# A kernel of delta rule, attention and experts on one core: more gathers of experts in the second block's delta rule

## The chip, the core and the metric

The kernel runs on one core of a Trainium2 chip. The core has a matrix engine (TensorE, in the profile PE), a vector engine (VectorE, DVE), a scalar engine (ScalarE, ACT), GpSimd (POOL), a queue engine (SyncE, SP), and 16 DMA engines that move data between main memory and the on-chip memory. The metric is the time of one execution on the device in microseconds, the median of several.

## What is computed

One layer over 1024 tokens of width 1024, float32. Its core, cut from the reference:

```python
proj = h @ w_in
y_a = _gdn_branch(gq, gk, gv, gz, ga, gb, ...)      # conv, delta rule in chunks, gated norm
y_b = _fox_branch(fq, fk, fv, ff, f_bias, w_out_fox)  # attention with forget gates, causal
mix = sigmoid(gate_a) * y_a + sigmoid(gate_b) * y_b
h = _layernorm(DEEPNORM_ALPHA * h + mix @ w_o, ln1_g, ln1_b)
h = _layernorm(DEEPNORM_ALPHA * h + _peer(h, peer_wq, peer_keys, peer_u, peer_v), ln2_g, ln2_b)

# _peer: each token chooses 8 heads x 16 = 128 of 16384 experts by top-k of product keys
u = jnp.take(u_tab, e_blk, axis=0)
act = jax.nn.gelu(jnp.einsum('td,tkd->tk', h_blk, u)) * g_blk
vv = jnp.take(v_tab, e_blk, axis=0)
return jnp.einsum('tk,tkd->td', act, vv)
```

Each of the 1024 tokens reads 128 rows of `u_tab` and 128 rows of `v_tab`, 4 KB each: 1.07 GB in all.

## The kernel before

**Blocks and units.** The sequence is worked on in four blocks of 256 tokens (`T`, `NB`), each two tiles of 128. What a block needs is cut into units, and `order()` (line 48) writes them out in one list, `UNITS`, of 548 pairs of a name and a number. For a block `b` they are: the projections (`sm`, `sv`, 13 `conv`, `z`, `rT`, `fqk`, `fv`); the delta rule (`nrm`, then for each of two chunks of 128 tokens `prod`, six levels `lev`, `wu`, `ws`, `o`, and `og`); attention (17 times `att` and `ato`, then `ot`); the merge (8 `mix`, 4 `wo`, 2 `ln`); and the choosing of the experts (8 heads, each two `top`, a `cand` and a `sel`, then `idx`). From block 1 on the delta rule, attention and merge of a block follow each other, and the projections of block `b + 1` stand between the units of the choosing of block `b`. Every engine walks through `UNITS` in the same order and does its part of each unit; semaphores tie them together.

**The experts beside it.** The experts of a block are worked on while later blocks are computed. A *dot* is one gather of 128 rows of `u_tab` (one expert choice of each token of a tile, 0.5 MB) by POOL, line 640, and one operation of VectorE that multiplies the rows with `h_cur` and sums them, line 999 (shown as a custom operation and a short read of the accumulator). A tile has 128 dots, the kernel 1024. A *token* is one gather of the 128 rows of `v_tab` of one token, line 652; TensorE sums four tokens at once with 8 matrix multiplications of 512 columns, line 1312. There are 1024 tokens too. Tokens of a tile may begin only when all its dots are done, its activations are made and turned over (line 1302).

**The ring.** Both kinds of gather write into a ring of 15 places (`NR`). POOL issues them in one fixed order and waits at each for the place to be free, that is, for the dot or the four tokens that used it 15 places before. So POOL runs at most 15 gathers ahead of VectorE and TensorE. Before a dot of a new head POOL also waits for that head's choice (`s_sel`, raised by line 1281 in `sel`). Between a unit's own instructions and the next unit's, VectorE does the unit's dots and TensorE its tokens, in order, waiting for each row to arrive.

**The table.** `pace()` (line 93) decides before the program is built how many dots (`DOTS`) and tokens (`TOKS`) stand behind each unit. Up to `idx` of block 0 dots are given out evenly. From there up to the last block's choosing, each unit has a share, `SHARE[kind]`, a guess of how long it takes, made larger for attention of later blocks by `share()`; the dots of that part of the program are handed out in proportion to the shares' running sum, so all shares together always receive the same number of dots. The result is cut off at what has been chosen: no dot of a block is placed before the unit `sel` of its second head, and 16 more with each further `sel`; no more than 8 dots follow a unit:

```python
            run += share(kind, b) if n < alone else 0.0
            want = base + round((T * (NB - 1) - base) * run / total)
        dots.append(max(dots[-1], min(want, ready, dots[-1] + 8)))
```

Tokens follow the dots at a distance of `P + LAG` = 136, in fours. The remaining units' table, and the part behind the last block's choosing, come from the same function.

Of the kernel before, what the change touches and what calls it, by code (L numbers as in the profile page):

```python
# [48 lines left out]
def order():  # L49
# [19 lines left out]
    for b in range(NB):  # L69
# [4 lines left out]
        for n, (kind, i) in enumerate(CHOOSE):  # L74
# [9 lines left out]
SHARE = {"sm": 1.0, "sv": 7.0, "nrm": 6.0, "conv": 3.5, "z": 5.0, "rT": 1.5, "fqk": 3.5, "fv": 5.0, "prod": 12.0, "lev": 5.0, "wu": 4.0,  # L84
         "ws": 3.0, "o": 4.0, "og": 8.0, "att": 2.5, "ato": 1.5, "ot": 4.0, "mix": 9.0, "wo": 6.0, "ln": 9.0,
         "top": 3.5, "cand": 6.5, "sel": 6.5, "idx": 3.0}


def share(kind, b):
    return SHARE[kind] * (1.0 + 0.7 * b if kind in ("att", "ato") else 1.0)  # L90


def pace():

    first = UNITS.index(("idx", 0, 0))
    last = UNITS.index(("idx", NB - 1, 0))
    alone = UNITS.index(("top", NB - 1, 0))
    total = sum(share(kind, b) for kind, b, i in UNITS[first + 1:alone])
    dots, toks = [0], [0]
    ready, run, lately = 0, 0.0, 0  # L100
    for n, (kind, b, i) in enumerate(UNITS):

        if kind == "sel":
            ready, lately = T * b + TOPK * i, 0
        if kind == "idx" and b:
            ready = T * (b + 1)
        if n == first + 1:
            ready, base = T, dots[-1]
        lately += 1
        if n <= first:  # L110
            want = max(0, ready - TOPK) + round(TOPK * lately / 7) if ready else 0
            want = min(want, P - 8)
        else:
# [4 lines that stand above are left out]
# [1579 lines left out]
```

How the kernel before makes its waits and increments, by code:

```python
            def sm_(b, i):  # L434
                sp.wait_ge(s_proj, projected(b, "sm", 0))
                next_items(b, 0, 1)
# [1 line left out]
            def conv(b, c):  # L438
                if c < 12:
                    sp.wait_ge(s_proj, projected(b, "conv", c))
                    next_items(b, 1 + c, 1)
                if b == 0 and c in (9, 11):
                    fetch("gt", (c - 9) // 2)
                if c == (3 if b else 9):
                    sp.wait_ge(s_rows, b + 1)
                    sp.dma_start(d_rows[:, b * T:(b + 1) * T], rows).then_inc(s_rowst, 16)
# [1 line left out]
            def z(b, i):  # L449
                sp.wait_ge(s_proj, projected(b, "z", i))
                next_items(b, 13 + 2 * i, 2)
# [1 line left out]
            def fqk(b, c):  # L453
                sp.wait_ge(s_proj, projected(b, "fqk", c))
                next_items(b, 17 + c, 1)
# [7 lines left out]
            def rT(b, i):  # L463
                sp.wait_ge(s_rowst, 16 * (b + 1))
                for j in range(2):
                    sp.wait_ge(s_mix[j], 4 * b)
                gates(TT * b)
# [1 line left out]
            def gt(b, m):  # L469
                i, k = divmod(m, 2)
                if k:
                    sp.wait_ge(s_gb2[i % 2], i // 2 + 1)
                    if i + 2 < 8:
                        fetch("gt", i + 2)
                    elif i == 7:
                        fetch("wo", 0)
# [1 line left out]
            def prod(b, c):  # L478
# [5 lines left out]
                    fetch("mix", 0)  # L484
                if c == 0 and b:
                    sp.wait_ge(s_proj, PB * (b + 1))
                    fetch("mix", 1)
```

## Time and profile before

| | us |
|---|---|
| median of 3 runs | 3906.41 |
| lowest, highest | 3903.19, 3912.52 |
| the profiled execution | 3916.44 |
| its span | 3914.4 |

The profile is of one execution, 10 us above the median. The span goes from the first to the last instruction, and windows are cut in it by times from its start. Busy times are sums over an engine's instructions; the DMA share is the mean busy share of the 16 DMA engines; a gather is one DMA on queue q0. Some shares stand at 1.01 to 1.03, since they are made from the packets' own times.

### The profile page before, as it was taken

To read this page: it belongs to the slowest core of one execution; us is meant where nothing else is said; L and a number is where in the kernel's file an instruction comes from. 1 tells how busy PE (TensorE), PEld (TensorE's weight loads), DVE (VectorE), ACT (ScalarE), POOL (GpSimd) and SP (SyncE) were. 2 spreads that over 40 slices of the span, in tenths; PEclk is the share of its full clock that TensorE was granted. 3 is DMA by queue.
4 is the path that set the end of the run, shared out by engine and by line. 5 is a ranking of instruction groups with operands and counts; after the bars stand their busy time and mean duration, and the time that the engine had idled before them with its cause. 6 is when DMAs were issued, how large, how long until landed. Compare 5 with 4: busy or idle time off the path is not lost.

```text
span 3914.4 us, 36529 instructions
## 1 busy us (share of the span) xinstructions
PE 2497.4 (64%) x11992; PEld 1538.0 (39%) x11992; DVE 2256.2 (58%) x5313; ACT 533.9 (14%) x1224; POOL 2304.5 (59%) x2086
## 2 busy tenths in 40 slices
PE   8788864567967876557967866556787710132354
PEld 6675752434735533334635533323554300000010
DVE  5243899754468776654368776555446668544300
ACT  3220310211003202111003202111101000000000
POOL 1000455367656666677556766577666677777765
PEclk9898987776988988777988988767898855555577
DMA  5213788599998999899998999899999999999998
GB/s 174 77 68 146 278 327 284 167 329 379 412 365 341 374 408 369 295 367 365 415 365 346 406 408 342 296 359 343 376 412 381 381 327 369 362 358 363 362 368 319
DMA packets 367619, 1290.18 MB, mean 330 GB/s; under 512 B 39468, under 2 KB 68148, under 8 KB 362308
## 3 DMA queue, kind: packets, MB, share of 16 engines
q0 software_dynamic: 294912, 1073.87, 72.6%
q1 hardware_dynamic: 66760, 201.39, 14.0%
q10 hardware_dynamic: 5760, 12.59, 0.8%
q8 instruction: 97, 1.59, 0.2%
q14 instruction: 90, 0.74, 0.0%
HBM read 1274.72 MB, written 12.98 MB: 329 GB/s over the span
## 4 chain that ended last, share of the span: by engine, by line
PE 26%; POOL 22%; DVE 15%; issue 14%; DMA 10%; another core or an unknown queue 7%; DVEq 3%; ACT 3%; SPq 0%; ACTq 0%; POOLq 0%
POOL ring L640 12%; POOL ring L652 11%; PE banks L1323 10%; DMA ring<-in_ev,idxT 8%; DVE ring L999 7%; PE banks L1312 5%; PE banks L1333 4%; PE banks L1588 2%; PE banks L1534 1%; PE banks L1373 1%; PE banks L1328 1%; PE banks L1514 1%; DVE arena L951 1%; DVE arena L953 1%
## 5 line engine op out<-in xcount | busy, mean ns | idle before, releaser
L640 POOL DMA_INDIRECT ring<-in_eu,eidx x1024 | 1188.2, 1160 | 1121.7 <-DVE eidx L1281 397.8
L999 DVE CUSTOM_DVE_ANT_0 ring<-ring,h_cur 128x1024 f32<-128x1024 f32 x1024 | 1216.7, 1221 | 293.1 <-DMA ring<-in_eu,eidx 266.3
L652 POOL DMA_INDIRECT ring<-in_ev,idxT x1024 | 1104.5, 1079 | 465.8 <-issue 298.2
L1312 PE MATMUL banks<-ring,wide 128*32 128x512 f32 x4096 | 718.2, 832 | 630.8 <-DMA ring<-in_ev,idxT 539.9
L1323 PE MATMUL banks<-arena,wslot 128*128 128x256 f32 (+1 forms) x3248 | 758.7, 391 | 64.5 <-ACT arena L752 30.2
L1323 PEld LDWEIGHTS banks<-arena,wslot 128*128 128x128 f32 (+1 forms) x3248 | 626.7, 195 | 229.4 <-issue 121.8
L1312 PEld LDWEIGHTS banks<-ring,wide 128*32 128x32 f32 x4096 | 146.5, 135 | 1045.3 <-issue 1003.5
L1333 PE MATMUL banks<-arena 128*128 128x128 f32 x1408 | 225.4, 321 | 55.0 <-ACT arena L801 30.5
L1333 PEld LDWEIGHTS banks<-arena 128*128 128x128 f32 x1408 | 205.9, 229 | 86.5 <-ACT arena L801 39.4
L1328 PE MATMUL banks<-ident,arena 128*128 128x128 f32 x216 | 50.9, 393 | 177.2 <-DVE arena L970 52.1
L1323 PE MATMUL banks<-ring,wslot 128*128 128x256 f32 (+1 forms) x656 | 152.3, 389 | 11.4 <-DMA wslot<-in_w_sm 7.0
L1534 PE MATMUL banks<-arena 128*128 128x64 f32 x528 | 93.5, 343 | 78.8 <-ACT arena L852 43.2
L982 DVE SCALAR_TENSOR_TENSOR h_cur<-h_cur,banks 128x512 f32<-128x512 f32 x16 | 10.3, 682 | 224.4 <-PE banks L1312 200.5
L1323 PEld LDWEIGHTS banks<-ring,wslot 128*128 128x128 f32 (+1 forms) x656 | 126.4, 196 | 30.1 <-issue 11.9
L1534 PEld LDWEIGHTS banks<-arena 128*128 128x128 f32 x528 | 85.7, 251 | 124.0 <-issue 72.4
L1200 DVE TENSOR_TENSOR arena<-arena,banks 128x256 f32<-128x256 f32 x48 | 18.1, 419 | 197.7 <-issue 91.9
L1173 DVE RECIPROCAL rinv<-rsum 128x1 f32<-128x1 f32 x64 | 10.5, 164 | 208.7 <-PE banks L1534 132.8
L1302 PE MATMUL banks<-ident,wgt 128*128 128x128 f32 x8 | 2.7, 342 | 196.8 <-issue 193.1
L1328 PEld LDWEIGHTS banks<-ident,arena 128*128 128x128 f32 x216 | 36.4, 201 | 201.0 <-DVE arena L970 60.2
L1588 PE MATMUL banks<-wslot,arena 128*128 128x512 f32 x256 | 113.5, 601 | 1.5 <-issue 1.5
L1514 PE MATMUL banks<-arena 65*128 65x512 f32 (+3 forms) x160 | 87.5, 670 | 29.3 <-DMA arena<-d_fv 25.6
L945 DVE MAX8 arena<-arena 128x8 f32<-128x128 f32 (+1 forms) x192 | 55.4, 289 | 73.0 <-ACT arena L897 64.4
(231 smaller groups left out, 2387.6 us busy)
## 6 DMA issues: line engine op xcount, KB each, us to landing
wslot<-in_w_pq SPq DMA_DIRECT2D x64, 576.0 KB
wslot<-in_w_mix SPq DMA_DIRECT2D x24, 1536.0 KB
wslot<-in_w_qkv SPq DMA_DIRECT2D x48, 512.0 KB
wslot<-in_w_fqk SPq DMA_DIRECT2D x32, 512.0 KB
wslot<-in_w_out SPq DMA_DIRECT2D x8, 2048.0 KB
ring<-in_eu,eidx POOLq DMA_INDIRECT x1024
ring<-in_ev,idxT POOLq DMA_INDIRECT x1024
wslot<-in_w_z SPq DMA_DIRECT2D x16, 512.0 KB
```

Source lines behind the costliest of these rows:

```text
L640: pool.indirect_dma_start(out=ring[:, UPOS[k] % NR, :], out_offset=None, in_=eu, in_offset=bass.IndirectOffsetOnAxis(ap=eidx[:, n % (2 * T ...
L652: pool.indirect_dma_start(out=ring[:, VPOS[k] % NR, :], out_offset=None, in_=ev, in_offset=bass.IndirectOffsetOnAxis(ap=idxT[:, n % (2 * T ...
L945: dve.max(v16[:, 0:8], vals)
L951: dve.max(v16[:, 8:16], vals)
L999: dve.tensor_tensor_reduce(out=row, in0=row, in1=h_cur[:, n % 3, :], scale=1.0, scalar=0.0, op0=ALU.mult, op1=ALU.add, accum_out=dots[:, n ...
L1312: last = pe.matmul(BY[k][32 * j:32 * j + 32, :], wide32[:, at:at + 32], ring[:, VPOS[4 * q + j] % NR, k * 512:(k + 1) * 512], start=(m == ...
L1323: last = pe.matmul(bank, w[:, k0 + k, :], rhs[:, k, :], start=(k == 0), stop=(k == nk - 1))
L1328: last = pe.transpose(bank[:, h * P:(h + 1) * P], src[:, h, :], ident[:, :])
L1333: last = pe.matmul(bank[:, h * P:(h + 1) * P], lhs[:, h, :], rhs[:, h, :], start=True, stop=True)
L1514: last = pe.matmul(SB[b][r][:, k0:k1], qa[b][0:FD + 1, j, qt * P:(qt + 1) * P], kh[b][0:FD + 1, i % 2, j, k0:k1], start=True, stop=True)
L1534: last = pe.matmul(TB[b][0][:, 0:FD], pT[b][:, k, :], vh[b][:, i % 2, k, FD * j:FD * (j + 1)], start=(k == 0), stop=(k == nk - 1))
L1588: last = pe.matmul(B[4 + tt][:, :], mixT[:, k, tt * P:(tt + 1) * P], w[:, k, :], start=(k == 0), stop=(k == KB - 1))
```

## The change

`share()` multiplies the shares of six kinds of units by 1.8 where the block is block 1: `prod`, `lev`, `wu`, `ws`, `o` and `og`, which is all of the delta rule but `nrm`.

```diff
 def share(kind, b):
+    if b == 1 and kind in ("prod", "lev", "wu", "ws", "o", "og"):
+        return SHARE[kind] * 1.8
     return SHARE[kind] * (1.0 + 0.7 * b if kind in ("att", "ato") else 1.0)
```

Since this raises the total, the rest gets a little less. All computed work is the same; the units' order is the same; what changes is behind which unit dots and tokens stand, and with it the order of POOL's gathers and the places in the ring. The tables, by stage:

| stage | units | dots, tokens before | dots, tokens after |
|---|---|---|---|
| up to `idx` of block 0 | 177 | 101, 0 | 101, 0 |
| block 1: delta rule with `nrm` | 23 | 49, 12 | 81, 44 |
| block 1: attention | 35 | 45, 44 | 43, 44 |
| block 1: merge | 14 | 43, 44 | 31, 32 |
| block 1: choosing, with block 2's projections | 61 | 101, 100 | 105, 104 |
| block 2: delta rule | 23 | 48, 48 | 46, 44 |
| block 2: attention | 35 | 64, 64 | 60, 60 |
| block 2: merge | 14 | 43, 44 | 41, 44 |
| block 2: choosing, with block 3's projections | 61 | 101, 100 | 96, 96 |
| block 3: delta rule | 23 | 48, 48 | 46, 44 |
| block 3: attention | 35 | 82, 84 | 77, 76 |
| block 3: merge | 14 | 43, 44 | 41, 44 |
| behind it | | 256, 392 | 256, 392 |

The cut at what has been chosen now takes hold in two places. Behind the third `wo` of block 1 the table has 256 dots, all of block 0; it has no dot and no token behind the next 14 units, up to block 1's second `sel` (before: 27 dots and 28 tokens). Until block 1's choosing ends the table then has 16 dots with each `sel`, 8 behind it and 8 behind the unit after it for most heads, and tokens in fours behind these two units and the two after them, then nothing to the next `sel`. In block 2 the 512th dot stands behind the first `cand`, the next 8 units have none, and for three heads the dots stand bunched in the same way.

TensorE, block 1's delta rule from the second chunk's `prod` on. L1333 (L1335 in the changed program, whose lines lie two further on) is a level's multiplication, L1302 turns the activations of tile 0 over, L1312 (L1314) is four tokens. Before:

```order
L1333 MATMUL banks<-arena 128x128 x36
L1302 MATMUL banks<-ident,wgt 128x128
L1312 MATMUL banks<-ring,wide 32x512 x8
L1333 MATMUL banks<-arena 128x128 x16
L1312 MATMUL banks<-ring,wide 32x512 x8
L1333 MATMUL banks<-state,arena 128x128 x4
```

and now:

```order
L1335 MATMUL banks<-arena 128x128 x8
L1304 MATMUL banks<-ident,wgt 128x128
L1314 MATMUL banks<-ring,wide 32x512 x8
L1330 MATMUL banks<-ident,arena 128x128 x4
L1335 MATMUL banks<-arena 128x128 x12
L1314 MATMUL banks<-ring,wide 32x512 x8
L1335 MATMUL banks<-arena 128x128 x12
L1314 MATMUL banks<-ring,wide 32x512 x8
L1330 MATMUL banks<-ident,arena 128x128 x4
```

The first tokens stand six units earlier, behind the second `prod`, and a group of four stands behind all but one of the units from there to the end of the delta rule, eleven in all where there were three.

VectorE, from the last `wo` of block 1 into its first `ln`. L1210 (L1212) adds the output projection, L957 to L970 (L959 to L972) are the layer norm, L999 (L1001) a dot, L989 (L991) the gates on tile 1's activations. Before:

```order
L1210 SCALAR_TENSOR_TENSOR arena<-arena,banks 128x512
L999 ISA ring,dots<-ring,h_cur 128x1024
L999 ISA dots 128x1
L999 ISA ring,dots<-ring,h_cur 128x1024
L999 ISA dots 128x1
L957 BN_STATS arena<-arena 128x6 x2
L959 BN_AGGR arena<-arena 128x2
L961 TENSOR_SCALAR arena<-arena 128x1
L964 RECIPROCAL arena<-arena 128x1
L966 TENSOR_SCALAR arena<-arena 128x1024
L968 TENSOR_TENSOR arena<-arena 128x1024
L970 TENSOR_TENSOR arena<-arena 128x1024
```

and now:

```order
L1212 SCALAR_TENSOR_TENSOR arena<-arena,banks 128x512
L991 TENSOR_TENSOR wgt<-wgt,gate 128x128
L959 BN_STATS arena<-arena 128x6 x2
L961 BN_AGGR arena<-arena 128x2
L963 TENSOR_SCALAR arena<-arena 128x1
L966 RECIPROCAL arena<-arena 128x1
L968 TENSOR_SCALAR arena<-arena 128x1024
L970 TENSOR_TENSOR arena<-arena 128x1024
L972 TENSOR_TENSOR arena<-arena 128x1024
L959 BN_STATS arena<-arena 128x6 x2
L961 BN_AGGR arena<-arena 128x2
```

The dots behind `wo` are gone, and the norm of the first tile is followed by that of the second with no dots between.

## Rows read from the trace of the kernel before

**Rows 1.** The page: span, DMA slices, the gathers' queue, issues of L640
```profile
span 3914.4 us, 36529 instructions
...
DMA  5213788599998999899998999899999999999998
...
q0 software_dynamic: 294912, 1073.87, 72.6%
...
L640 POOL DMA_INDIRECT ring<-in_eu,eidx x1024 | 1188.2, 1160 | 1121.7 <-DVE eidx L1281 397.8
```

**Rows 2.** Windows at the stages: engines' busy us, clock, DMA share, GB/s
```profile
core 0: us, PE busy (x) PEld busy (x) DVE busy (x) ACT busy (x) POOL busy (x), PEclk, DMA share, GB/s
679.00:830.00 151.00, 86.22 (x489) 69.83 (x489) 107.00 (x198) 36.48 (x80) 71.08 (x57) 0.76 0.61 203
830.00:960.00 130.00, 94.84 (x384) 44.83 (x384) 72.88 (x155) 21.02 (x54) 99.18 (x89) 0.63 1.00 374
...
1201.00:1477.00 276.00, 213.97 (x973) 132.07 (x965) 206.45 (x598) 52.08 (x130) 183.88 (x164) 0.89 0.98 385
1477.00:1647.00 170.00, 102.44 (x632) 69.49 (x632) 106.52 (x196) 37.26 (x81) 113.29 (x100) 0.80 0.90 328
...
2523.00:2783.00 260.00, 153.00 (x757) 79.12 (x761) 130.52 (x240) 40.36 (x76) 181.62 (x159) 0.72 0.94 339
```

**Rows 3.** Windows: the two halves of block 1's delta rule
```profile
679.00:747.00 68.00, 40.73 (x224) 33.81 (x224) 51.17 (x90) 16.18 (x36) 32.09 (x24) 0.80 0.58 185
747.00:830.00 83.00, 45.49 (x268) 36.01 (x265) 55.83 (x109) 20.30 (x45) 38.99 (x33) 0.73 0.64 218
```

**Rows 4.** Timeline, a level step: VectorE, then gather issues on POOL
```profile
717.05 0.69 DVE L1126 TENSOR_TENSOR arena<-arena,banks 128x512 f32<-128x512 f32 x1
...
718.85 1.22 DVE L999 CUSTOM_DVE_ANT_0 ring<-ring,h_cur 128x1024 f32<-128x1024 f32 x1
...
720.00 1.22 DVE L999 CUSTOM_DVE_ANT_0 ring<-ring,h_cur 128x1024 f32<-128x1024 f32 x1
...
721.32 0.69 DVE L1126 TENSOR_TENSOR arena<-arena,banks 128x512 f32<-128x512 f32 x1
...
718.06 0.94 POOL L640 DMA_INDIRECT ring<-in_eu,eidx  x1 [0.30 <-issue]
720.35 1.68 POOL L640 DMA_INDIRECT ring<-in_eu,eidx  x1 [1.35 <-DVE dots L999]
```

**Rows 5.** POOL in block 1's second prod; window with VectorE at rest
```profile
758.82 1.68 POOL L640 DMA_INDIRECT ring<-in_eu,eidx  x1 [10.46 <-DVE dots L999]
...
3800.00:3900.00 100.00, 52.40 (x280) 10.89 (x272) 0.00 (x0) 0.00 (x0) 62.37 (x67) 0.72 0.97 366
```

**Rows 6.** Timeline of VectorE: wo and sel of blocks 0 and 1
```profile
358.63 0.69 DVE L1210 SCALAR_TENSOR_TENSOR arena<-arena,banks 128x512 f32<-128x512 f32 x1 [6.18 <-PE banks L1588]
...
445.60 0.18 DVE L1281 SCALAR_TENSOR_TENSOR eidx<-arena 128x32 uint32<-128x32 f32 x1
...
672.79 0.18 DVE L1281 SCALAR_TENSOR_TENSOR eidx<-arena 128x32 uint32<-128x32 f32 x1
...
1091.67 0.69 DVE L1210 SCALAR_TENSOR_TENSOR arena<-arena,banks 128x512 f32<-128x512 f32 x1 [2.74 <-PE banks L1588]
...
1206.44 0.19 DVE L1281 SCALAR_TENSOR_TENSOR eidx<-arena 128x32 uint32<-128x32 f32 x1
...
1470.57 0.18 DVE L1281 SCALAR_TENSOR_TENSOR eidx<-arena 128x32 uint32<-128x32 f32 x1
```

**Rows 7.** Windows before the second sel, blocks 0, 0, 1 and 2
```profile
337.00:412.00 75.00, 59.75 (x206) 38.41 (x207) 29.19 (x87) 6.37 (x12) 0.00 (x0) 0.89 0.37 138
412.00:446.00 34.00, 24.27 (x102) 20.36 (x101) 27.32 (x93) 14.07 (x36) 14.36 (x15) 0.90 0.84 317
1092.00:1206.00 114.00, 74.72 (x356) 47.03 (x349) 86.48 (x230) 17.07 (x36) 63.54 (x56) 0.82 0.88 342
2007.00:2089.00 82.00, 55.95 (x273) 38.18 (x272) 63.89 (x194) 14.48 (x30) 44.70 (x41) 0.83 0.85 331
```

## The prediction

> **What bounds the kernel now.** I read the page first: the DMA slices and the queues [rows 1]. The gathers of expert rows (queue q0, 2048 of 0.5 MB each) take 72.6% of 16 engines' span, the DMA slices stand at 9 or more for most of the run, and no compute engine does. 72.6% of 3914.4 us over 2048 gathers is 1.39 us of all 16 DMA engines for one gather; that price carries the sum. The chain of waits mixes the vector engine, the gathers and the matrix engine, so I did not sum by it.
>
> Then the windows, cut at the program's stages [rows 2]. Where the share is about 1.0 the transfers set the time: block 1's attention (89 gathers in 130 us, 1.46 us each with the key and value loads) and the choosing of block 1 (0.98). The delta rule of block 1 is the exception: 61 gathers (49 dots, 12 tokens by the table; POOL, running ahead, has 57 in the window) in 151 us, share 0.61. Cut in two [rows 3], its halves have 0.58 and 0.64, so the engines idle 68 x 0.42 = 28.6 us and 83 x 0.36 = 29.9 us. As the bytes of the program don't change, the change in time is the change in the DMA engines' idle time, as long as some stretch stays transfer-bound. That is the account I keep; a sum stage by stage stands beside it.
>
> **The change, part by part.** The table puts 32 more dots and 32 more tokens into the delta rule of block 1; every one is taken from a later stage. Nothing else is added.
>
> *First half of the delta rule* (units nrm to o of chunk 0): 36 dots instead of 22, no tokens. In a level step the vector engine is nearly full: three operations of 0.6 to 0.7 us and two dots, 4.27 us from one L1126 to the next [rows 4], so a third dot of 1.15 us (start to start of consecutive dots, [rows 4]) comes on top. In prod it waits for the norm and some are hidden. 14 x 1.15 = 16 us is the ceiling, I take 11. DMA work there is 68 x 0.58 = 39.4 plus 14 x 1.39 = 19.5, in 79 us: idle 20, a gain of 9.
>
> *Second half*: 89 gathers (45 dots, 44 tokens) instead of 39. POOL enters with the ring of 15 places full and leaves some 8 places short, so about 81 x 1.39 = 113 us of transfers fall here, more than the 83 us there are. The second prod's wait for its gate rows stays, with the ring full and POOL waiting 10.46 us for a dot [rows 5]: some 10 us idle, and 4 for gaps. POOL itself costs more here. A gather's issue takes 0.94 us where VectorE does its small operations and 1.68 under dots [rows 4], with 0.30 between issues, and 62.37 / 67 = 0.93 where VectorE does nothing [rows 5]. With 45 dots of 1.15 us in some 130 us, 40% of the time is under dots: 0.94 + 0.4 x 0.74 + 0.30 = 1.54 us an issue, 81 of them 125 us, 12 more than their transfers. Part of that runs during the wait; I take 8. So 135 us, idle 22, a gain of 8. The lower bound of idle is 0, the upper is that of block 2's delta rule, 170 x 0.10 = 17, plus 10 and 12. Matrix work is no limit: eight more groups of tokens. Together the delta rule grows by 11 + 52 = 63 us and saves 17 us of idle time.
>
> *What is late next.* The dots can't run ahead of the experts chosen. All 256 dots of block 0 are now done with unit wo 2 of block 1, and dots of block 1 come no sooner than its second sel: 14 units without a gather, where 27 dots and 28 tokens stood. POOL's next gather waits for the first sel (L1281). What such a stretch looks like is in the trace, since block 0 has the same units with no gathers at all: from its third wo to its second sel 358.6 to 445.6, 87 us; in block 1 1091.7 to 1206.4, 114.8 us [rows 6]. DMA idles from where POOL has run out, 15 places or 21 us ahead of the dots. For block 0 that window, 337 to 412, has share 0.37 of weights and stores alone: idle 75 x 0.63 = 47. After the first sel POOL fills the ring, 15 gathers, and stops: 412 to 446 has exactly that, share 0.84, idle 5. Block 1 now idles 114 x 0.12 = 14 there [rows 7]. The loss is 52 - 14 = 38 us (bounds 25, if block 1's weights fill more than block 0's, and 48).
>
> *Bursts.* From there to the end of block 1's choosing the table has 16 dots and 16 tokens for each sel, in two units with 8 dots and 4 tokens each and two with 4 tokens, then four units with none. Between the second and the eighth sel are six such periods in 264 us now [rows 6], with 155 gathers. Share 0.98 x 264 = 259 less 155 x 1.39 = 215 leaves 44 us for weights. With 192 gathers: 267 + 44 = 311, less 15 fetched ahead, plus some 8 at the end: 301 us, 50 a period. The vector engine needs about 38 (six of block 0's periods, 16 dots each, take 227.2 us, from its second sel at 445.6 to its eighth at 672.8 [rows 6]), so it isn't the bound, and DMA finds a free place nearly always: between bursts it has 8 tokens and 15 dots' places to fill, 32 us of work in some 20. POOL has 32 issues of 1.24 and 16 dots over them at up to 0.74 more, 51 us a period, as long as the transfers: that and the transfers' bursts won't fit without gaps. Idle 0 to 20 more, I take 8.
>
> *Block 2's choosing* meets the ceiling too: 512 dots are done with its first cand, 508 before ln ends. Eight units have no gathers. By the same reckoning 20 us idle before its first sel and 5 after, against 82 x 0.15 = 12 now [rows 7]: a loss of 13 (5 to 20).
>
> *The stretches behind it* lose 46 gathers in all up to the last block's choosing (dots and tokens: block 2's delta rule 2 and 4, attention 4 and 4, merge 2 and 0, its choosing 5 and 4; block 3's delta rule 2 and 4, attention 5 and 8, merge 2 and 0). Where the share is 1.0 each gives back 1.39. In the delta rules it gives less: from 61 gathers in block 1 to 96 in block 2 the delta rule grows from 151 to 170 us [rows 2], some 0.53 a gather. I take 6 us as lost that way (0 to 12). From the last block's choosing on, the table is the same.
>
> *Sum*: -17 (delta rule) +38 +8 +13 +6 = **+48 us** of idle time. Stage by stage: +63 delta rule, +6 attention (89 to 87 gathers, which no longer starts with a full ring), -5 merge, -27 the stretch without gathers, +37 six periods, +10 the last units, -64 for 46 gathers later, +6 +13 as above: +39. The second counts no gaps in the bursts; I take **+41**. The profiled execution took 3916.4 us with a span of 3914.4; the median of three is 3906.4. On the median the forecast is 3947.
>
> One price could be read otherwise. The rows show 1.39 us of DMA time for a gather, and 374 GB/s at a share of 1.00 [rows 2]. The Trainium skill, DMA: Bandwidth & Descriptors, "Anatomy of one DMA", fits a transfer's time as 2.0 us plus bytes over 436 GB/s, so 1.20 us a gather beyond the fixed part; by that estimate the burst periods and the second half of the delta rule would be some 50 us cheaper and the later gathers worth 9 less, and the time would come to about 3905. No stretch of gathers alone reached that rate.
>
> **Rivals.**
> *A, faster: cheap where added, dear where removed.* If the delta rule stays bound by its chain, an added gather costs 0.53 there as between block 1 and block 2 [rows 2]: 64 x 0.53 = 34 instead of 63. The periods of choosing are 37.9 us with 16 gathers and 44 with 25.8, 0.65 a gather, so 37 more cost 24 and not 37. And block 3's attention takes 260 us for 166 gathers, 1.57 each, so 46 fewer give back 72 and not 58. That is -29 -13 -14 = -56: 3891. Against it: 89 gathers in the second half want 113 us of transfers in 83. It decides if the delta rule stays under 185 us and the periods under 48.
> *B, no change: cheap both ways.* As A, but the gathers removed give back no more than 58: 3905.
> *C, POOL becomes the bound.* If nearly every issue of the second half fell under a dot, 1.98 us each, 89 would last 176 us, 41 more than I count: 3988. Against it: dots take 40% of that time, not all. The Trainium skill, SBUF — State Buffer, "SBUF: two separate sides", says that VectorE and GpSimd share a pair of ports under an exclusive lock, held for the whole instruction when an operation reads two operands in SBUF, so that gather descriptors can't be written meanwhile. The rows agree (1.68 beside 0.94). By that rule it is the bunched dots after each sel that hold POOL up most; the sum has it with 8 us in the delta rule and within the 8 of the bursts, and without it would be some 12 us less.
> That the change doesn't move what it says is excluded by the order of instructions.
>
> **How the numbers follow.** The forecast has 0.71, A 0.12, B 0.12, C 0.05. Within the forecast the bounds of the terms (delta rule 17 us each way, first hole -13 to +10, bursts -8 to +12, second hole 8, relief 6), which won't all fall one way, give 3916 to 3980. The range must take in most of B: 3900 to 3982 leaves out about 2 in 10. A measurement of this kernel tells 0.2%, 8 us: faster 0.12, same 0.12, slower 0.76.
>
> **What would show it.** In the profile after, the delta rule of block 1 should last some 214 us with a DMA share near 0.8; a hole of 50 to 60 us should stand between the merge and the first sel of block 1 with a share below 0.5 and no POOL work; POOL should wait for L1281's successor there, 50 us or more (now it waits so only once, at the start, 397.8 us with everything before it [rows 1]); the six periods should be 50 us with a share near 1.0; the last block's choosing and the tail should be as before, only later. The forecast is wrong if the delta rule stays near 170 us, if the hole is filled by weights, or if the periods stay at 44 us.

## The result, and the profile after

| | before | after |
|---|---|---|
| median, us | 3909.47 (4 runs) | 4033.54 (4 runs) |
| lowest, highest | 3903.19, 3914.89 | 4016.74, 4041.02 |
| span of the profiled execution | 3914.4 | 4014.3 |

The change makes the kernel slower by 2.9%: ratio 1.0292, interval 1.0257 to 1.0328. The forecast was 3947 with a range that ended at 3982: the direction was right and the size was not (124 us by the medians, 41 forecast). The profile of after is of its fastest run, so the spans differ by 100 us where the medians differ by 124; what follows explains the 100.

The page of after (lines stand two further on), to be read beside [rows 1]:

```profile
span 4014.3 us, 36522 instructions
...
DMA  5214887899968999989996999899999999999998
...
q0 software_dynamic: 294912, 1073.87, 71.5%
q1 hardware_dynamic: 66760, 201.39, 14.0%
...
L642 POOL DMA_INDIRECT ring<-in_eu,eidx x1024 | 1173.2, 1146 | 1170.3 <-DVE eidx L1283 506.9
```

The bytes are the same, but 71.5% of 4014.3 us is 2870 us of gathers where it was 2842 (72.6% of 3914.4): their transfers took longer. POOL waits 507 us for choices, where it was 398. The windows of after at the stages (columns as in [rows 2]), in this order: block 1's delta rule; its two halves; attention; the stretch without gathers; from first to second sel; the six periods between block 1's second and eighth sel; block 2's choosing with the units before it:

```profile
679.00:893.50 214.50, 115.15 (x617) 79.68 (x617) 143.87 (x262) 36.41 (x80) 150.42 (x118) 0.73 0.82 286
679.00:762.00 83.00, 45.11 (x224) 37.80 (x224) 67.50 (x122) 19.40 (x40) 52.31 (x37) 0.73 0.68 224
762.00:893.00 131.00, 70.04 (x393) 41.88 (x393) 75.86 (x140) 17.01 (x41) 97.65 (x81) 0.73 0.91 325
893.50:1031.00 137.50, 89.96 (x384) 41.87 (x384) 70.73 (x152) 20.91 (x54) 103.46 (x93) 0.65 1.01 376
...
1137.00:1213.00 76.00, 61.05 (x231) 37.47 (x230) 35.15 (x98) 7.96 (x14) 0.86 (x1) 0.89 0.45 172
1213.00:1248.00 35.00, 21.52 (x95) 16.43 (x93) 27.79 (x95) 13.77 (x33) 14.31 (x15) 0.87 0.80 305
1247.00:1578.00 331.00, 209.96 (x963) 125.63 (x964) 216.81 (x611) 40.07 (x108) 209.57 (x192) 0.79 0.95 354
2113.00:2483.00 370.00, 268.15 (x1201) 169.21 (x1193) 259.02 (x769) 60.61 (x152) 204.16 (x190) 0.85 0.89 337
```

Below, stages are cut at marks that hold no dot (the vector engine's norm, output gate, merge and sel operations), so that they compare between kernels; such a cut may lie some us from the windows above. "Idle" is a stretch less the mean time that the 16 DMA engines' packets took in it.

| stage | before, us (idle) | after, us (idle) | change | forecast |
|---|---|---|---|---|
| block 1: delta rule | 143.6 (57) | 203.2 (37) | +60 | +63 |
| attention | 152.8 (0) | 164.7 (0) | +12 | +6 |
| merge to second sel | 228.3 (11) | 198.3 (50) | -30 | -32 |
| six periods of choosing | 264.1 (5) | 330.9 (17) | +67 | +37 |
| rest of it | 9.1 | 16.1 | +7 | +10 |
| block 2 and 3, to the last block's first sel | 1496 | 1482 | -13 | -45 |
| behind it | 939 | 937 | -2 | 0 |

The first three rows came within 6 us of the forecast. POOL on the timeline of after, at the stretch without gathers, shows the wait that was forecast at "50 us or more", then 15 issues without a pause, of which the second stands here, then the wait for a dot of the second sel:

```profile
1213.89 0.94 POOL L642 DMA_INDIRECT ring<-in_eu,eidx  x1 [76.02 <-DVE eidx L1283]
1215.13 0.94 POOL L654 DMA_INDIRECT ring<-in_ev,idxT  x1 [0.30 <-issue]
...
1249.15 1.68 POOL L654 DMA_INDIRECT ring<-in_ev,idxT  x1 [16.69 <-DVE dots L1001]
```

The two misses are the six periods and the return from later stages. In the periods, the waits of before (1206 to 1470) and of after (1247 to 1578), columns: what waited for what, us in total, times, longest:

```profile
PE banks L1312 <- DMA ring<-in_ev,idxT: 27.2, 5, 8.8
...
DVE ring L999 <- DMA ring<-in_eu,eidx: 23.5, 9, 6.7
```

```profile
PE banks L1314 <- DMA ring<-in_ev,idxT: 99.5, 13, 21.4
...
DVE ring L1001 <- DMA ring<-in_eu,eidx: 52.1, 18, 7.6
POOL ring L642 <- PE banks L1314: 33.9, 5, 10.1
...
POOL ring L654 <- DVE dots L1001: 24.8, 4, 16.7
```

The matrix and vector engines wait 101 us more for rows. POOL's waits for free places grow less: before, three such rows come to 41 us (20.3, 11.3 and 9.2); after, the two shown and one of 1.7 come to 60, and 16.7 of these lie ahead of the window, being the wait that ends at 1249.15. In the first period, right behind the hole, TensorE's tokens wait for rows longest:

```profile
1264.21 3.64 PE L1314 MATMUL banks<-ring,wide 128*32 128x512 f32 x16 [21.37 <-DMA ring<-in_ev,idxT]
```

### The profile page after: what moved, and what is told of

Same layout as the page of the kernel before. It is cut to its first block, busy times and chain, and to the rows that moved or that the text cites. A ratio compares the mean times of both kernels' runs of the same rounds, so it can differ in the third digit from the quotient of the medians.

```text
span 4014.3 us, 36522 instructions
## 1 busy us (share of the span) xinstructions
PE 2532.4 (63%) x11992; PEld 1554.8 (39%) x11992; DVE 2257.2 (56%) x5313; ACT 523.2 (13%) x1217; POOL 2297.8 (57%) x2086
## 3 DMA queue, kind: packets, MB, share of 16 engines
q0 software_dynamic: 294912, 1073.87, 71.5%
## 4 chain that ended last, share of the span: by engine, by line
PE 32%; POOL 20%; DVE 15%; issue 13%; another core or an unknown queue 8%; DMA 7%; DVEq 3%; ACT 2%; ACTq 0%; SPq 0%; POOLq 0%
PE banks L1325 14%; POOL ring L654 10%; POOL ring L642 10%; DVE ring L1001 7%; PE banks L1314 6%; DMA ring<-in_ev,idxT 5%; PE banks L1335 4%; PE banks L1590 2%; PE banks L1375 2%; PE banks L1536 1%; DMA ring<-in_eu,eidx 1%; PE banks L1364 1%; PE banks L1330 1%; PE banks L1516 1%
## 5 line engine op out<-in xcount | busy, mean ns | idle before, releaser
L642 POOL DMA_INDIRECT ring<-in_eu,eidx x1024 | 1173.2, 1146 | 1170.3 <-DVE eidx L1283 506.9
L1001 DVE CUSTOM_DVE_ANT_0 ring<-ring,h_cur 128x1024 f32<-128x1024 f32 x1024 | 1215.6, 1222 | 363.2 <-DMA ring<-in_eu,eidx 315.1
L1314 PE MATMUL banks<-ring,wide 128*32 128x512 f32 x4096 | 732.0, 836 | 659.2 <-DMA ring<-in_ev,idxT 596.0
L1314 PEld LDWEIGHTS banks<-ring,wide 128*32 128x32 f32 x4096 | 147.3, 136 | 1086.8 <-issue 1070.0
L1335 PE MATMUL banks<-arena 128*128 128x128 f32 x1408 | 234.9, 330 | 71.2 <-ACT arena L803 27.7
L1335 PEld LDWEIGHTS banks<-arena 128*128 128x128 f32 x1408 | 214.9, 238 | 108.0 <-issue 54.0
L984 DVE SCALAR_TENSOR_TENSOR h_cur<-h_cur,banks 128x512 f32<-128x512 f32 x16 | 10.2, 681 | 206.8 <-PE banks L1314 172.9
L1590 PE MATMUL banks<-wslot,arena 128*128 128x512 f32 x256 | 112.2, 595 | 2.9 <-issue 2.9
L1375 PE MATMUL banks<-wslot,arena 128*128 128x512 f32 x192 | 90.7, 631 | 20.1 <-ACT arena L754 20.1
```

The costliest lines, as they stand in the source:

```text
L642: pool.indirect_dma_start(out=ring[:, UPOS[k] % NR, :], out_offset=None, in_=eu, in_offset=bass.IndirectOffsetOnAxis(ap=eidx[:, n % (2 * T ...
L1001: dve.tensor_tensor_reduce(out=row, in0=row, in1=h_cur[:, n % 3, :], scale=1.0, scalar=0.0, op0=ALU.mult, op1=ALU.add, accum_out=dots[:, n ...
L1314: last = pe.matmul(BY[k][32 * j:32 * j + 32, :], wide32[:, at:at + 32], ring[:, VPOS[4 * q + j] % NR, k * 512:(k + 1) * 512], start=(m == ...
L1335: last = pe.matmul(bank[:, h * P:(h + 1) * P], lhs[:, h, :], rhs[:, h, :], start=True, stop=True)
L1375: last = pe.matmul(PN[b][tt][:, :], xTs[b][:, k, tt * P:(tt + 1) * P], w[:, kk, :], start=(k == 0), stop=(k == KB - 1))
L1590: last = pe.matmul(B[4 + tt][:, :], mixT[:, k, tt * P:(tt + 1) * P], w[:, k, :], start=(k == 0), stop=(k == KB - 1))
```

## The experiments

They ran in three groups, on chips numbered 1, 11 and 4; the number of the first result's chip isn't known. The kernel before was run in each group: medians 3769, 3775 and 3773 us, single runs 3751 to 3791, which is 3.5% less than above. Ratios are to before in the same group. e1 to e4 ran on chip 1, the copies of both kernels and the short dots on 11, e5 and the other factors on 4. There is one profile a kernel, and before's is of chip 11, so stage lengths are mostly compared across chips. How far such a comparison carries: e3_bunched has before's table up to the second sel, and its first three stages differ from before's by 2 to 5 us.

> The kernel before, once more, for its stages on the chip of these runs: each stage in the same proportion as in its first profile, the delta rule of block 1 near 0.7 of the change's.

> The change, once more, beside its variants: 1.029 times the kernel before, as first measured, within 0.005.

Before's span was 3780.1. The change's ratio was 1.021 (1.0166 to 1.0255): the loss is smaller here, 79 us by the medians, and the expectation (1.024 to 1.034) missed. All stages of the table keep their signs. In these profiles the change has (before, after): delta rule 140.7, 194.8; attention 144.0, 155.1; six periods 250.2, 308.4; blocks 2 and 3 1439, 1419.

Counted by the bytes that arrived in each stage, this is where the gathers went and what they cost there. The delta rule got 55 more and took 54 us more, 1.0 each. The stretch from merge to the second sel got 54 fewer and gave back 35 us, 0.65 each. The six periods got 28 more and took 58 us more, 2.1 each. Blocks 2 and 3 got 42 fewer and gave back 20 us, 0.5 each. The other 14 (in attention and behind the periods) took 22 us. So no place that lost gathers gave back as much for one as any place that got them took.

**Is it the hole, or the gathers beside the delta rule?** e1_local gives the delta rule as many gathers, taken from block 1's own attention and merge, so that there is no long stretch without (its table meets the ceiling for the two units before the second sel) and the periods stay nearly as even as before:

```diff
+    if b == 1 and kind in ("prod", "lev", "wu", "ws", "o", "og"):
+        return SHARE[kind] * 1.8
+    less = 0.64 if b == 1 and kind in ("att", "ato", "ot", "mix", "wo", "ln") else 1.0
+    return less * SHARE[kind] * (1.0 + 0.7 * b if kind in ("att", "ato") else 1.0)
```

> The delta rule of block 1 has 85 dots and 48 tokens beside it as in the change, but they are taken from the attention and the merge of the same block, so that 242 dots are done at its end (before 238, the change 256) and the ceiling of chosen experts is never met. Theory 1, the loss lies in the hole and the bursts that the ceiling makes: without them the filled idle time of the delta rule is a gain of some 20 us, 3885 to 3895. Theory 2, gathers in the delta rule are dear themselves (its chain is longer, VectorE's dots hold POOL up): 3935 or more, since the delta rule grows by 64 us and attention and merge give back only what their own chains allow.

Ratio 1.0127 (1.0103 to 1.0152): slower with hardly a hole, as the second theory had it. The delta rule went from 140.7 to 210.8 us, attention from 144.0 to 146.2, and from there to the second sel 235.6 us became 210.8. Attention, of before and of e1_local:

```profile
821.00:965.00 144.00, 108.32 (x452) 54.01 (x452) 78.56 (x166) 25.96 (x63) 113.47 (x99) 0.67 1.01 381
```

```profile
892.00:1039.00 147.00, 105.89 (x404) 58.52 (x404) 63.88 (x139) 26.07 (x63) 77.36 (x75) 0.59 0.91 322
```

It issues 24 gathers fewer and is not shorter; its share has fallen to 0.91. So its share of 1.0 [rows 2] didn't mean that fewer gathers would make it shorter: something else took as long. That this was attention's own chain is likely, but no run shows it by itself. The granted clock is lower in e1_local (0.59 against 0.67), and attention's own 260 matmuls kept TensorE busy for 76 us instead of 67; how much the stage would give back at the same clock is open.

**The other side of that point.** e4_hole leaves the delta rule nearly as it was (46 dots, 8 tokens) and loads attention and merge, so that the hole and the bursts are as in the change:

```diff
+    more = 1.42 if b == 1 and kind in ("att", "ato", "ot", "mix", "wo", "ln") else 1.0
+    return more * SHARE[kind] * (1.0 + 0.7 * b if kind in ("att", "ato") else 1.0)
```

> The kernel before, with 46 dots and 8 tokens in block 1's delta rule, and the attention and merge of block 1 made to take 34 dots and tokens more than now, so that the ceiling is met behind the same unit as in the change, with the same hole, the same bursts and nearly the same table behind them. Theory 1, hole and bursts are the loss and the delta rule's filling a gain of 20: 4035 to 4060, slower than the change. Theory 2, the delta rule is the loss: 3920 to 3960.

Ratio 1.0283 (1.025 to 1.0315), more than the change's 1.021; neither theory's range was met, the first was the nearer. Its attention:

```profile
822.00:1020.00 198.00, 117.73 (x516) 54.35 (x516) 95.72 (x195) 25.96 (x63) 150.71 (x132) 0.66 1.00 372
```

33 gathers more cost 54 us, 1.64 each. The delta rule is the cheaper place for them, by 0.7% of the kernel (the two intervals just touch, and the runs are of two chips). What the two kernels share is the hole and the bursts: in both the six periods and what is behind them to block 2 take more than before, 69 us in the change and 77 here. In e1_local, which shares neither, this is 7 us, and it loses less than either.

**The bursts.** e2_even is the change with the dots at the ceiling handed out two behind each unit. e3_bunched is the kernel before with block 1's dots bunched behind each sel from the third on. Its table has 137 gathers in the six periods where before has 155; most of the rest stand behind the last sel.

```diff
             want = base + round((T * (NB - 1) - base) * run / total)
+            if kind in CHOOSING and dots[-1] < want:
+                want = max(dots[-1], min(want, ready - TOPK + 2 * lately))
```

```diff
             want = base + round((T * (NB - 1) - base) * run / total)
+            if CHOSEN < n < alone and 310 > n and kind in CHOOSING:
+                behind = UNITS[n - 1][0] == "sel"
+                want = want if kind == "sel" or behind else dots[-1]
```

> The change with the same hole of 14 units, but the dots behind it are handed out two to a unit at the ceiling, not eight and eight behind each sel; tokens follow evenly. Theory 1a, the bunching makes the six periods 55 us instead of 50: they come to 50 or less and the whole is 30 to 45 us faster than the change, 3985 to 4000. Theory 1b, the load alone (32 gathers a period) makes them 55: no change against it, 4025 to 4035.

> The kernel before, with its own table up to block 1's second sel; from there to the end of block 1's choosing the same 13 dots a period are bunched behind each sel and the unit after it. Theory 1a, bunching itself costs about 5 us a period, engines taking turns: 3930 to 3945. Theory 1b, it costs nothing while there are only 26 gathers a period: 3905 to 3915.

e2_even: 1.0176 (1.0129 to 1.0223). e3_bunched: 1.0085 (1.0052 to 1.0117). The six periods in before, the change, e2_even and e3_bunched:

```profile
1201.00:1451.00 250.00, 193.28 (x917) 123.98 (x918) 197.12 (x577) 45.85 (x117) 172.90 (x157) 0.89 1.02 404
```

```profile
1230.00:1538.00 308.00, 207.49 (x977) 125.72 (x978) 217.23 (x610) 41.50 (x110) 207.72 (x191) 0.81 0.97 373
```

```profile
1232.00:1519.00 287.00, 214.80 (x971) 127.59 (x973) 217.88 (x608) 43.58 (x111) 208.52 (x185) 0.87 1.01 399
```

```profile
1200.00:1451.00 251.00, 188.95 (x886) 122.58 (x885) 185.28 (x556) 46.10 (x119) 149.00 (x142) 0.87 0.97 370
```

Of the 58 us that the periods grow, 37 remain when the same gathers are even (share 1.01: it is the transfers), and 21 are due to the bunching. The 21 show in two ways: 12 us are idle DMA time, and 9 are more time in transfers, most of it dearer gathers: 1.364 us each against 1.329 even and 1.320 before. In e3_bunched the six periods take 251.4 us, as before, but with 13 gathers fewer by the bytes: 12 us of idle DMA time came in, and a gather took 1.364 us instead of 1.320, 6 us together. So bunching cost some 18 us there too, at 23 gathers a period, 3 us a period where the first theory had 5. The price shows behind the eighth sel, 18.5 us more for the 10 gathers left over and other transfers. By the medians e3_bunched loses 30 us, within the range of the first theory; the second (no cost at 26 gathers a period) fell. The gain of e2_even over the change in the medians (1.0176 against 1.021, 13 us where 30 to 45 were expected) is within the intervals; its 21 us are read from the stage of one profile each.

TensorE's clock can be left out as the cause of the longer periods. The granted clock of the stage is lower in the change than in before (0.81 and 0.89, means over the levels of 1.2 and 2.4 GHz), but the rows have 0.212 us of busy time for a matmul in the one (207.49 for 977) and 0.211 in the other (193.28 for 917), and the stage's matmuls other than the tokens' kept TensorE busy for 146 and 148 us.

**Is it the vector engine's dots?** In b_short_dots (before) and a_short_dots (the change) a dot covers 256 of the 1024 columns; the rest of the product is left out.

```diff
-                        out=row, in0=row, in1=h_cur[:, n % 3, :], scale=1.0, scalar=0.0,
+                        out=row[:, 0:256], in0=row[:, 0:256], in1=h_cur[:, n % 3, 0:256], scale=1.0, scalar=0.0,
```

> The kernel before with each dot's operation on VectorE over 256 of the 1024 columns (the rest of the product is left out; gathers and everything else stay). VectorE's part of a dot falls from 1.22 to some 0.4 us. Theory of transfers: most stages are bound by them, the time falls by 1 to 3%. Theory of VectorE: choosing and delta rule are bound by its dots, and POOL's issues by them: over 5%.

> The change with the same short dots. If the change loses because its bunched and added dots fill VectorE and hold up POOL's issues, it is less than 1.5% slower than the kernel before with short dots. If it loses by the hole and by gathers that arrive too late for engines that work in order, it stays 2.5 to 3.5% slower than that.

Ratios to before: 0.952 (0.949 to 0.955) and 0.9714 (0.9685 to 0.9743). One over the other is 1.020, the same loss as with full dots, so it doesn't come from their length. It lies between the two ranges expected for it (under 1.5%, 2.5 to 3.5%), and the gain of before, 4.8%, between its two as well (1 to 3%, over 5%). The page of b_short_dots, POOL's issues and the dots:

```profile
L640 POOL DMA_INDIRECT ring<-in_eu,eidx x1024 | 989.4, 966 | 1164.5 <-DVE eidx L1281 397.1
...
L999 DVE CUSTOM_DVE_ANT_0 ring<-ring,h_cur 128x256 f32<-128x256 f32 x1024 | 406.6, 424 | 590.0 <-DMA ring<-in_eu,eidx 589.0
```

The mean issue is 0.966 us instead of 1.160 [rows 1]. In the delta rule of the change the issues take 1.25 us in the mean with full dots and 0.97 with short ones, and the stage grows by 54 us with the former and by 41 with the latter: POOL's hold-up and the dots' own time are at most 13 of the 54. The rest is transfers that found no idle time: they grow by 74 us with full dots and by 65 with short ones, while idle DMA time falls by only 20 and 24.

**Dots or tokens?** e5_dots_only is e1_local with the tokens of the delta rule held at 12:

```diff
+        if WAITED[0] < s <= WAITED[1] and toks[-1] >= 12:
+            ready = toks[-1]
         if toks[-1] % P == 0 and dots[s - 1] < edge:
             ready = toks[-1]
```

> Block 1's delta rule gets 85 dots as in e1_local, but its tokens stay at 12 as in the kernel before; attention has 29 dots and 64 tokens, merge 27 and 28, nothing behind changes by more than 2, and there is no unit without gathers but where the kernel before has them. e1_local (85 dots, 48 tokens) lost 53 us: its delta rule grew by 70 us, attention by 2, merge and what is before the first sel shrank by 18. Theory 1 (what is added to the delta rule costs about 1 us each whatever it is, and what is removed from attention gives nothing back): 36 dots add 25 to 35 us to the delta rule, attention has 93 gathers instead of 89 and grows by 6, merge gives back 20: 15 to 20 us slower, ratio 1.004 to 1.005. Theory 2 (the tokens are what makes the second half slow, since the matrix engine waits for rows between the level steps): the delta rule grows by 15 us or less, ratio 0.998 to 1.001. Rival (dots cost most, tokens ride along): the delta rule grows by 50 us or more and the ratio is 1.010 or above.

Ratio 1.0087 (1.006 to 1.0115), above what the first theory gave and below the rival's. Its delta rule is 172.9 us: 36 dots add 32 us, and the 36 tokens of e1_local 38 more. A dot costs 0.9 there and a token 1.05, so the first theory holds for this stage. Part of the 32 us may be TensorE: the delta rule's own matmuls kept it busy for 93 us at a granted clock of 0.67, and in before for 80 at 0.74 (in the change for 82 at 0.73). But its attention takes 177.4 us, 33 more than before where 6 were expected:

```profile
681.00:854.00 173.00, 99.45 (x486) 82.46 (x487) 139.30 (x256) 34.30 (x76) 117.23 (x86) 0.67 0.77 259
854.00:1031.00 177.00, 125.86 (x528) 61.98 (x532) 62.45 (x137) 26.10 (x63) 110.77 (x106) 0.63 0.96 358
```

The table has 93 gathers behind its units, but POOL issues 106: in the delta rule it issued 86 where the table has 97, so it left that stage with its lead spent, as in the change (109 of 125), and made it up in attention. The change issues 106 in attention too and takes 155 us. The traces settle part of the 22 us between them: by the bytes 109 gathers arrive there and 101 in the change, which with their price is 12 us, and 8 us are idle DMA time. The table has 64 tokens there instead of 44, and attention's own matmuls took 74 us instead of 63, at a granted clock of 0.63 instead of 0.69; whether either of these makes the stage longer stays open.

**How it grows.** The change's factor of 1.8 was set to 1.2, 1.4 and 0.8.

```diff
-        return SHARE[kind] * 1.8
+        return SHARE[kind] * 1.2
```

> The change with factor 1.2 in the place of 1.8: delta rule of block 1 with 57 dots and 20 tokens (8 and 8 more than before), four units without a gather ahead of the second sel, no bunching beyond the first two periods. Theory 1 (each gather beside the delta rule costs about 1 us and gives back 0.3): 16 x 0.7 = 11 us, ratio 1.003 (1.001 to 1.005), delta rule 155 us. Theory 2 (the loss begins only where the hole and the bursts are, the delta rule has free transfer time): ratio 0.996 to 1.000, delta rule below 149 us.

> Factor 1.4: delta rule with 65 dots and 28 tokens (16 and 16 more), eight units without a gather ahead of the second sel, three periods of block 1's choosing bunched, four units without in block 2. Theory 1: 32 x 0.7 = 22 us for the delta rule, some 6 for the smaller hole: ratio 1.007 (1.004 to 1.010). Theory 2 (loss from hole and bursts only): delta rule below 158 us, ratio 1.000 to 1.003. Rival (loss is a threshold of a full ring and comes with 1.8 alone): ratio below 1.000.

> The other direction, factor 0.8: delta rule of block 1 with 40 dots and 4 tokens (9 and 8 fewer), attention 46 and 44, merge 44 and 44, block 1's choosing 102 and 104, a few more in each stage behind it. Theory 1 (beside block 1's delta rule a gather costs about 1 us even at the table of before, and elsewhere it costs nothing while attention is at its own chain): faster, ratio 0.995 to 0.999. Theory 2 (the first gathers beside the delta rule are nearly free, its 0.61 share being real free time, and those that move behind it cost 1.39 each): slower, 17 x (1.39 - 0.5) = 15 us, ratio 1.002 to 1.006.

| factor | gathers beside the delta rule | delta rule, us | six periods, us | blocks 2 and 3, us | ratio |
|---|---|---|---|---|---|
| 0.8 | 44 | 130.0 | 256.3 | 1448 | 1.0042 (1.002 to 1.0064) |
| before | 61 | 140.7 | 250.2 | 1439 | 1 |
| 1.2 | 77 | 154.9 | 264.7 | 1425 | 1.0038 (1.0021 to 1.0056) |
| 1.4 | 93 | 171.2 | 287.7 | 1423 | 1.0068 (1.0047 to 1.0089) |
| 1.8 | 125 | 194.8 | 308.4 | 1419 | 1.021 (1.0166 to 1.0255) |

With 1.2 and 1.4 the first theory held in size, and with 1.2 in the delta rule's length. With 0.8 it fell and the second held (1.002 to 1.006 expected): the 17 gathers taken out give back 11 us in the delta rule, 0.6 each, and the periods, what is behind them and the later blocks take 24 more. So of the five values tried the kernel before has the lowest time, and the loss grows slowly at first: 0.4% with a hole of four units and 2.1% with one of 14. Blocks 2 and 3 return less and less of what is moved ahead of them: 14 us for the first 14 gathers (1.2), 16 for 23 (1.4), 20 for 46 (1.8).

## Why the prediction missed

**What held.** The delta rule was to grow by 63 us with a share near 0.8, and grew by 60 with 0.82. Its two halves were put at 79 and 135 us, and windows of 83 and 131 show them. The stretch from merge to the second sel was to shrink by 32 and shrank by 30; its hole has share 0.45, where below 0.5 was forecast, and POOL's wait of 76 us is there. The idle DMA time was to grow by 48; summed over all packets it grew from 486 to 541 us, by 55. The rivals are ruled out: A and B needed the delta rule under 185 us, C needed 176 in its second half, which took 131.

**The premise that failed: "the change in time is the change in the DMA engines' idle time".** The same bytes took 45 us more of DMA time (3429 to 3474 us over all packets); on the page q0 accounts for 28 of them and q1 for 14. The prediction put this term at nothing. It is the largest part of the miss: the profiled executions differ by 100 us where 41 were forecast, and of the 59 between, 45 are dearer transfers, 7 are idle time beyond the 48, and 7 are the step from the sum of 48 down to 41. The prediction priced every gather at one mean, 1.39 us. By stage, before, it is 1.34 in the periods, 1.37 in attention, 1.43 in block 2's delta rule and 1.57 beside block 1's, where the queue is least full. The rows showed it: 57 gathers at 0.61 of 151 us [rows 2] are 1.6 each. The change moves gathers from the first kind of place to the last, and makes the good places dearer: the periods' gathers went to 1.40 and block 2's from 1.32 to 1.38, some 20 us together. In the experiments the bunched periods were dearer than the even ones by 0.035 a gather. What in the transfers takes the longer time isn't settled. In these runs gathers are dearer in stages where the queue runs empty and is then filled at once; that the one causes the other wasn't tested.

**The six periods, 331 us instead of 301.** Two terms. I took 15 gathers off as "fetched ahead" and put some 8 on at the end; but each period ends with the ring filled for the next, as it began, and the window has 192 issues, all that the table gives. Their transfers with the weights' took 314 us where I had about 301. And in the sum stage by stage I counted no gaps: idle time there is 17 us, 12 more than before, within the bounds of the first sum (0 to 20), and left out of the second, which the forecast followed. Here the step that failed is "DMA finds a free place nearly always". A place comes free only when its dot is done or its four tokens are summed, and both wait in order: POOL waited 16.7 us for a dot at the second sel, and the tokens behind it 21 us for their rows [the rows of 1249.15 and 1264.21 above].

**The return, 13 us instead of 45.** Attention of blocks 2 and 3 did give back for 21 gathers: 23 us here, 27 in the experiments' copies, where the price of 1.39 gives 29. The delta rules did not: 6 gathers fewer in each of two gave back nothing in sum here (+4 and -3); they had some 18 us of idle time each. I had 6 us for that. Block 2 from its last wo to block 3's nrm grew by 22 us (14 in the copies) where the forecast, 13 less 12.5 for its 9 gathers, had none. The 106 us from wo to the second sel, with the hole in them and fewer gathers, became 90, but its six periods grew by 40, 18 of them idle DMA time: for three heads the dots stand bunched as in block 1, and I had priced the hole alone.

**And the median.** The medians differ by 24 us more than the profiled executions. Runs of the changed kernel lie up to 24 us apart, of before in the experiments up to 37 on one chip, and the part behind the last sel, with the same table in every kernel, took 708 to 733 us there with full dots. What makes the runs differ, and whether the 24 us are more than that, stays open.

**What the share said.** I read 0.61 as free room that could take gathers at the cost of the other engines' waits. e1_local shows the account with hardly a hole: 70 us more in the delta rule, 18 less from attention to the first sel, and 9 less in blocks 2 and 3. In the copies 55 more gathers brought 74 us of DMA time into the delta rule, and only 20 of these came out of its 55 us of idle time. Idle DMA engines are no free room where the rows' own operations stand in order among those of the stage: the tokens alone made TensorE wait 26 us for rows in the delta rule of the change, and none in before. And a stretch at 1.0 need not get shorter with fewer gathers.

**The other price of a gather.** The prediction gave an estimate of 1.20 us a gather, worked out from the fit (2.0 us plus bytes over 436 GB/s) of the Trainium skill, DMA: Bandwidth & Descriptors, "Anatomy of one DMA", and with it 3905. No stage of over 30 us came under 1.30 in any run, so the measurement decides against it. The Trainium skill, SBUF — State Buffer, "SBUF: two separate sides", says that a VectorE operation with two inputs in SBUF and a GpSimd operation that reads SBUF lock one pair of ports against each other for the whole instruction. The short dots agree with it: issues of gathers, which read their indices from `eidx`, fell from 1.16 to 0.97 us in the mean when the operation beside them was a third as long. But the loss of the change didn't depend on it.

## What to carry to other kernels

Before gathers are moved into a stretch whose DMA engines idle, price both places by their own rows (share times length over the gathers in it), and ask of the place they leave whether its own chain is nearly as long: if it is, a share of 1.0 promises no return. Where work is bounded by what has been chosen, running ahead of the choice turns into a stretch with none and a crowded one behind it: here the first gave back 0.65 us for each gather that it lost, and the second took 2.1 for each that it got, 1.4 when they were spread evenly. Count a ring's lead at both ends of a window, and never take the sum that leaves out the gaps when another one has them.

## What the runs showed of the hardware

- The same gather took different DMA time by its surroundings. In the six periods of the experiments it was 1.32 us when steady and 1.36 when bunched. Beside block 1's delta rule, with shares of 0.52 to 0.84, it was 1.47 to 1.63 with full dots, and 1.37 in a_short_dots, where the share was 0.91.
- Shortening the vector engine's operation from 1.22 to 0.42 us brought POOL's mean gather issue from 1.16 to 0.97 us, and the whole kernel down 4.8%, though the matrix engine's work and the bytes were the same. Of the 189 us between the profiled executions 121 are idle DMA time and 69 are transfers that took less (3381 to 3312 us over all packets).
- The kernel before took 3909 us when the change was first measured and 3769 to 3775 in the three groups of experiments, 3.5% less; the part behind the last sel took 771 and 725 us in the two profiles of it, and the loss of the change was 2.9% and 2.1%. The chips of the three groups agree within 0.2%. Since the first result's chip isn't known, that chips differ by as much isn't shown.
